# Last mixer of a stacked-block kernel: the query products and their rotations move behind those of keys and values

## The chip, the cores and the metric

The kernel runs on one core of one Trainium2 chip, as one program and one launch. The metric is the device time of that launch in microseconds. Three unprofiled runs of the kernel before took 3191.38, 3191.89 and 3195.28 us, so its median is 3191.89 us.

## The reference, cut to what matters

Two stacks of two blocks each run one after the other on 256 tokens of width 1024, all in float32. The change touches only the mixer of the last block, `odd_mixer`:

```python
p = h @ w_in                                   # (256, 1024) @ (1024, 2608)
q, kc, vc, ks, vs, kw, vw, gl = split(p)       # q: 16 heads of 64; the six others: 4 heads of 64
q, kc, ks, kw = rope(q), rope(kc), rope(ks), rope(kw)
gates = sigmoid(gl)                            # 3 for each head and token
k_cmp = compress(kc, pos[0], w1[0], ...)       # blocks of 32 tokens, stride 16: 15 blocks
v_cmp = compress(vc, pos[1], w1[1], ...)       # gelu((blocks + pos) @ w1 + b1) @ w2 + b2
o = gates_0 * att(q, k_cmp, v_cmp) + gates_1 * att(q, ks, vs) + gates_2 * att(q, kw, vw)
y = o @ w_out
```

With 256 tokens every one of the 4 selection blocks is chosen and the window covers everything, so the second and third branch are plain causal attention. Behind the mixer stand the last mixture of experts and a final norm.

## The kernel before, in words

Activations lie transposed: 8 chunks of 128 features on the partitions, 256 tokens along the free axis. Weights stream from HBM through a ring of 7 slots of 2 MB. SyncE issues the loads in the order in which `block(...)` was called while the program was planned, each as soon as the block 7 places ahead of it in that order has been read (`free_slot`, then `load`, L974). PSUM banks are handed out at planning time too: `fill_turn` goes round banks 0 to 3 for products, and `fill(b)` takes one of banks 4 to 7 for rotations and doubled keys. Every engine has its program written out by hand and runs it in order; semaphores join them. No scheduler rearranges anything, so the order of the calls in the TensorE, ScalarE and VectorE functions is the order on the chip.

One `unit` (L1053) is the product of 256 output features with all 256 tokens: 32 matmul records. Two `token_unit`s (L1068) are the product of the same size with tokens on the partitions, for values. The six products of one 256-column part of the weights are: kc and vc (one block, `od2.kc`, `od2.vc`), and for each of the selected and the window branch (`od2.kv[0]`, `od2.kv[1]`) one key unit and two token units. The queries take four units from two blocks (`od2.q`).

For a unit that needs rotary embedding, ScalarE copies the product into `z` (L1693, L1958), TensorE multiplies it by a fixed rotation matrix (`rotate`, L1420, 2 records), and VectorE combines the two in three operations (`rotary`, L2376, L2378, L2380). The rotated keys of a branch are then doubled into both halves of the partitions by TensorE (L1618, two banks of 4 records each) and copied to `kT` by ScalarE (L1967).

The compressed branch: VectorE writes the overlapping blocks plus the position term into `cmp_blk`, for kc and then vc: four times one memset (L2579) and four additions (L2584). TensorE multiplies them by the two halves of `w1` for kc and then vc (L1630, 128 records each, 60 moving columns a record), ScalarE applies gelu (L1973), and TensorE makes the second product (L1640 for keys, L1646 and L1649 for values). Attention follows: 48 jobs (16 heads by 3 branches), L1097 scores, L1108 transposes, L1121 values on TensorE, with softmax on VectorE and ScalarE.

The order on TensorE before is: norm sums, four query units, kc, vc, `rotate` of the queries, key and value products of both branches, the 48-column gate product (L1608), `rotate` of kc, `rotate` of kv[0], doubling of kv[0], `rotate` of kv[1], doubling of kv[1], compression, attention. On VectorE it is: rotary of the queries, the gate mask (L2574), rotary of kc, the compressed branch's blocks, rotary of kv[0], rotary of kv[1], attention.

Of the kernel before, what the change touches and what calls it, by code (L numbers as in the profile page):

```python
# [31 lines left out]
T = 256  # L32
# [165 lines left out]
def stacked_blocks_kernel(nc, A, consts_dram, counts_dram, slots_dram, out):  # L198
    with ExitStack() as ctx:
# [117 lines left out]
        def con(name):  # L317
            at, n = CONST[name]
            return const[:, at:at + n]
# [11 lines left out]
        bank_full = [sem(f"bank_full{b}") for b in range(8)]  # L331
# [13 lines left out]
        proj_ready = sem("proj_ready")  # L345
# [7 lines left out]
        rope_ready = sem("rope_ready")  # L353
        dup_ready = sem("dup_ready")
# [139 lines left out]
        pairs = []  # L494
# [164 lines left out]
        for i in range(4):  # L659
            b = block(col_load(A["od_pw1_w"][0], i * T, T), col_load(A["od_pw1_w"][0], D + i * T, T, T))  # L660
# [37 lines left out]
        for i, cap in enumerate(CAPS):  # L698
# [10 lines left out]
            if paired:  # L709
                st = paired_steps(lambda s, n: ([moe_col(s * HSTEP)], [moe_col(E1_FF + s * HSTEP)]),  # L710
                                  lambda s, n: [moe_row(s * HSTEP)], (0, 3) if i < 6 else (), scatter_fills)
# [102 lines left out]
        def rope_linear(W, c0, n):  # L814
            st = linear(W, c0, n, proj_ready)
            st.rots = [fill(4 + i % 4) for i in range(len(st.units))]
            st.rope = count(rope_ready, len(st.units))
            return st
# [36 lines left out]
        od2 = Stage()  # L855
        od2.norm = norm(moe2[0].h)
        QW, KW = NSA_H * HD, NSA_KV * HD
        od2.q = rope_linear(W3, 0, QW)
        b = block(col_load(W3, QW))
        fs = [fill_turn((proj_ready, count(proj_ready, 1) + 1)) for _ in range(2)]  # L860
        b.release = (bank_full[fs[1].b], fs[1].n)
# [5 lines left out]
        for i in range(2):  # L867
# [8 lines left out]
            st.dup_fills = [fill(4 + g, (dup_ready, count(dup_ready, 1) + 1)) for g in range(2)]  # L876
            od2.kv.append(st)
        od2.gate_fill = fill_turn((gates_ready, 1))
        od2.blk = count(cmp_ready, 2)
        od2.cmp = []  # L880
        for i in range(2):
# [154 lines left out]
        def _(pe):  # L1036
            def open_bank(f):

                if f.before is not None:
                    pe.wait_ge(*f.before.freed)  # L1040
                return PSB[f.b]

            def landed(b):
                pe.wait_ge(slot_landed[b.slot], b.landed)

            def unit(b, u, f, x, ready=None):

                ps = open_bank(f)
                for c in range(2):
                    for k in range(KD):  # L1050
                        if ready is not None and c == 0:
                            ready(k)
                        mm = nc.tensor.matmul(ps[:, c * T:(c + 1) * T],  # L1053
                                              kblk(b)[:, k, u * T + c * P:u * T + (c + 1) * P], x[:, k, :],
                                              start=k == 0, stop=k == KD - 1)
                mm.then_inc(bank_full[f.b], 1)

            def pe_linear(st, x, ready):
                for i, (b, u, f) in enumerate(st.units):
# [18 lines left out]
            def normed(st):  # L1078
                return lambda k: pe.wait_ge(xn_ready, st.xn + k + 1)
# [335 lines left out]
            def rotate(st, at_chunk):  # L1415

                for i, f in enumerate(st.rots):
                    pe.wait_ge(proj_ready, st.done + i + 1)
                    ps = open_bank(f)
                    nc.tensor.matmul(ps[:], con("rot"), z[:, at_chunk + 2 * i:at_chunk + 2 * i + 2, :],  # L1420
                                     start=True, stop=True).then_inc(bank_full[f.b], 1)
# [169 lines left out]
            pe_experts(moe2[0])  # L1591

            pe_norm(od2.norm)
            pe_linear(od2.q, xn, normed(od2.norm))
            landed(od2.kc.units[0][0])
            unit(*od2.kc.units[0], xn)
            unit(*od2.vc.units[0], xn)
            rotate(od2.q, 0)
            for i, st in enumerate(od2.kv):
                b, u, f = st.ku  # L1600
                landed(b)
                unit(b, u, f, xn)
                for b, c, f in st.vu:
                    token_unit(b, c, f, xn, KW, KW)
            ps = open_bank(od2.gate_fill)
            for c in range(TC):
                for k in range(KD):
                    mm = nc.tensor.matmul(ps[:, c * 3 * NSA_H:(c + 1) * 3 * NSA_H], xn[:, k, c * P:(c + 1) * P],  # L1608
                                          gate_w[:, k, :], start=k == 0, stop=k == KD - 1)
            mm.then_inc(bank_full[od2.gate_fill.b], 1)  # L1610
            rotate(od2.kc, 8)
            for i, st in enumerate(od2.kv):
                rotate(st, 12 + 2 * i)
                pe.wait_ge(rope_ready, st.rope + 1)
                for u, f in enumerate(st.dup_fills):
                    ps = open_bank(f)
                    for o in range(2):
                        mm = nc.tensor.matmul(ps[:, o * T:(o + 1) * T], con(f"dup{o}"), z[:, 12 + 2 * i + u, :],  # L1618
                                              start=True, stop=True)
                    mm.then_inc(bank_full[f.b], 1)  # L1620
            for i, st in enumerate(od2.cmp):
                pe.wait_ge(cmp_ready, od2.blk + 2)
                for b in st.blocks:
# [27 lines left out]
                mm.then_inc(bank_full[st.ofill.b], 1)  # L1651
            pe.wait_ge(cmp_ready, od2.cmp[1].out + 1)
            pe.wait_ge(dup_ready, od2.kv[1].dup + 2)
            pe_attention(od2.att)
            pe_linear(od2.out, mixed, lambda k: pe.wait_ge(mix_ready, od2.att.mix + k + 1))
            pe_experts(moe2[1])
# [10 lines left out]
        def _(act):  # L1667
            def full(f):
                act.wait_ge(bank_full[f.b], f.n)
                return PSB[f.b]  # L1670
# [16 lines left out]
            def copy_units(st, dst):  # L1687
                for i, (b, u, f) in enumerate(st.units):
                    d = dst(i)
                    ps = full(f)[:, 0:2 * T]  # L1690
                    if len(d.shape) == 3:
                        ps = ps.rearrange("p (c t) -> p c t", c=2)
                    nc.scalar.copy(d, ps).then_inc(f.freed[0], 1)  # L1693

            def pairs(x, at_chunk=0):
                return lambda i: x[:, at_chunk + 2 * i:at_chunk + 2 * i + 2, :]
# [253 lines left out]
            act_experts(moe2[0])  # L1950

            normalise(od2.norm)
            copy_units(od2.q, pairs(z))
            copy_units(od2.kc, pairs(z, 8))
            copy_units(od2.vc, pairs(z, 10))
            for i, st in enumerate(od2.kv):
# [5 lines left out]
            full(od2.gate_fill)  # L1962
            nc.scalar.activation(gates.rearrange("p c n -> p (c n)"), PSB[od2.gate_fill.b][:, 0:TC * 3 * NSA_H], ACT.Sigmoid)\
                .then_inc(gates_ready, 1)
            for i, st in enumerate(od2.kv):
                for u, f in enumerate(st.dup_fills):
                    nc.scalar.copy(kT[:, 4 * i + 2 * u:4 * i + 2 * u + 2, :],  # L1967
                                   full(f).rearrange("p (c t) -> p c t", c=2)).then_inc(dup_ready, 1)
            for i, st in enumerate(od2.cmp):
                ps = full(st.hfill)  # L1970
                NB = NSA_KV * NCMP
# [21 lines left out]
        def _(dve):  # L1993
# [15 lines left out]
            def full(f):  # L2009
                dve.wait_ge(bank_full[f.b], f.n)  # L2010
                return PSB[f.b]
# [360 lines left out]
            def rotary(st, at_chunk):  # L2372

                for i, f in enumerate(st.rots):
                    x = z[:, at_chunk + 2 * i:at_chunk + 2 * i + 2, :]
                    nc.vector.tensor_tensor(rot_tmp, full(f).rearrange("p (c t) -> p c t", c=2), twice(con("sin")),  # L2376
                                            ALU.mult).then_inc(bank_free[f.b], 1)
                    chain(nc.vector.tensor_tensor(x, x, twice(con("cos")), ALU.mult))  # L2378
                    freed(f)
                    nc.vector.tensor_tensor(x, x, rot_tmp, ALU.add).then_inc(rope_ready, 1)  # L2380
                    dve.wait_ge(rope_ready, st.rope + i + 1)
# [185 lines left out]
            dve_experts(moe2[0])  # L2567

            normalise(od2.norm, lambda k: scol[:, 1, 0, k:k + 1], lambda k: mod[:, 1, 0, k:k + 1])
            rotary(od2.q, 0)  # L2570
            dve.wait_ge(gates_ready, 1)
            for c in range(TC):
                g0 = gates[:, c, 0:3 * NSA_H:3]
                step(nc.vector.tensor_scalar(g0, g0, con("cmprow")[:, c:c + 1], None, ALU.mult))  # L2574
            rotary(od2.kc, 8)
            for i, pos in enumerate(("pos_k", "pos_v")):
                for o in range(2):
                    half, other = slice(o * HD, (o + 1) * HD), slice((1 - o) * HD, (2 - o) * HD)
# [6 lines left out]
                                cmp_blk[i][half, ls, o, c, :], src[:, :, a:a + NCMP],  # L2585
                                col(pos, a * CMP_S, CMP_S)[half].unsqueeze(2).to_broadcast([HD, CMP_S, NCMP]), ALU.add)
                ins.then_inc(cmp_ready, 1)
            for i, st in enumerate(od2.kv):
                rotary(st, 12 + 2 * i)
            dve_attention(od2.att)  # L2590
            add_chunks([f for b, u, f in od2.out.units], lambda k: mod[:, 1, 2, k:k + 1], ALU.mult)
            dve_experts(moe2[1])
# [33 lines left out]
```

## Time and profile before

| what | value |
|---|---|
| median of the runs | 3191.89 us |
| profiled execution | 3207.41 us, with a span of 3205.6 us |
| mean granted TensorE clock | 0.929 |
| TensorE busy | 2880.0 us (90% of the span), 15071 matmul records |
| VectorE busy | 797.5 us (25%) |
| ScalarE busy | 394.8 us (12%) |
| HBM | 641.64 MB read, 200 GB/s over the span |
| first unit of the last mixer starts | 2542.38 us |
| first compression product starts | 2649.14 us |
| attention of the last mixer starts | 2710.49 us |

A granted clock of 1.00 is TensorE at 2.4 GHz and 0.50 is 1.2 GHz; a value between the two is a stretch that holds both. Times of day below are microseconds from the start of the span. Idle time counts only where it stands on TensorE, the engine that nearly all of the chain of waits runs through.

### The profile page before, as it was taken

To read this page: it belongs to the slowest core of one execution; us is meant where nothing else is said; L and a number is where in the kernel's file an instruction comes from. 1 tells how busy PE (TensorE), PEld (TensorE's weight loads), DVE (VectorE), ACT (ScalarE), POOL (GpSimd) and SP (SyncE) were. 2 spreads that over 40 slices of the span, in tenths; PEclk is the share of its full clock that TensorE was granted. 3 is DMA by queue.
4 is the path that set the end of the run, shared out by engine and by line. 5 is a ranking of instruction groups with operands and counts; after the bars stand their busy time and mean duration, and the time that the engine had idled before them with its cause. 6 is when DMAs were issued, how large, how long until landed. Compare 5 with 4: busy or idle time off the path is not lost. (4 is left out here: it accounts for less than half of the span.)

```text
span 3205.6 us, 35329 instructions
## 1 busy us (share of the span) xinstructions
PE 2880.0 (90%) x15071; PEld 2201.0 (69%) x15071; DVE 797.5 (25%) x1968; ACT 394.8 (12%) x997; POOL 53.7 (2%) x67
## 2 busy tenths in 40 slices
PE   3999999979899999999997887796899989997998
PEld 3767888757778888888862332565878668566786
DVE  1211211882220202021111000344223221643112
ACT  1102000112200000000000000122100101432001
POOL 0000000600000000000000000000000000000000
PEclk9999999989899999999998999888899985788999
DMA  7333256420388888888889999300669830005462
GB/s 240 131 119 118 95 194 207 174 79 1 131 312 323 298 320 300 321 299 321 300 323 394 394 394 393 114 1 3 215 211 327 255 95 1 1 1 175 142 236 92
DMA packets 328577, 645.02 MB, mean 201 GB/s; under 512 B 12875, under 2 KB 98273, under 8 KB 328417
## 3 DMA queue, kind: packets, MB, share of 16 engines
q1 hardware_dynamic: 318608, 636.51, 55.1%
q10 hardware_dynamic: 9809, 6.21, 0.7%
q8 instruction: 121, 1.98, 0.3%
q14 instruction: 39, 0.32, 0.0%
HBM read 641.64 MB, written 1.05 MB: 200 GB/s over the span
## 5 line engine op out<-in xcount | busy, mean ns | idle before, releaser
L1160 PE MATMUL bank<-xn,ring 128*128 128x128 f32 (+3 forms) x6208 | 829.7, 296 | 7.2 <-issue 6.8
L1160 PEld LDWEIGHTS bank<-xn,ring 128*128 128x128 f32 x6208 | 797.0, 192 | 54.3 <-issue 22.2
L1053 PE MATMUL bank<-xn,ring 128*128 128x256 f32 x2048 | 462.9, 390 | 54.2 <-DVE xn L2563 17.7
L1053 PEld LDWEIGHTS bank<-xn,ring 128*128 128x128 f32 x2048 | 401.8, 197 | 115.8 <-issue 41.1
L2139 DVE TENSOR_TENSOR att<-att,bank 128x128 f32<-128x128 f32 (+2 forms) x162 | 48.6, 301 | 841.0 <-ACT att L1756 841.0
L1189 PE MATMUL bank<-ring,att 128*128 128x512 f32 (+1 forms) x560 | 246.1, 594 | 0.0
L1206 PE MATMUL bank<-ring,xn 128*64 128x512 f32 x336 | 175.9, 675 | 64.8 <-issue 64.8
L1189 PEld LDWEIGHTS bank<-ring,att 128*128 128x128 f32 (+1 forms) x560 | 101.9, 186 | 121.6 <-issue 121.6
L1210 PE MATMUL bank<-ring,xn 128*64 128x512 f32 x336 | 176.3, 676 | 0.0
L1206 PEld LDWEIGHTS bank<-ring,xn 128*64 128x64 f32 x336 | 48.5, 154 | 169.6 <-issue 168.4
L1756 ACT ACTIVATE att<-bank 128x128 f32<-128x128 f32 (+2 forms) x162 | 46.6, 288 | 873.7 <-PE bank L1160 873.7
L1390 PE MATMUL bank<-ring,att 128*128 128x512 f32 (+2 forms) x320 | 140.7, 595 | 0.0
L2186 DVE SCALAR_TENSOR_TENSOR sq<-ring,cs,sq 128x512 f32<-128x512 f32 x168 | 126.3, 752 | 6.0
L1160 PEld LDWEIGHTS bank<-sq,ring 128*128 128x128 f32 x1024 | 115.4, 192 | 4.9 <-issue 4.9
L1160 PE MATMUL bank<-sq,ring 128*128 128x128 f32 (+1 forms) x1024 | 115.6, 275 | 1.2 <-DMA ring<-moe_w_up 1.2
L1390 PEld LDWEIGHTS bank<-ring,att 128*128 128x128 f32 (+2 forms) x320 | 54.0, 173 | 74.5 <-issue 74.4
L2358 DVE TENSOR_TENSOR att<-att,bank 128x256 f32<-128x256 f32 (+3 forms) x64 | 18.8, 294 | 344.9 <-ACT att L1835 344.8
L2479 DVE SCALAR_TENSOR_TENSOR att<-z,cols,att 128x256 f32<-128x256 f32 x210 | 103.1, 562 | 1.1
L1086 PE MATMUL bank<-sq,ones 128*128 128x256 f32 x224 | 57.5, 416 | 48.0 <-ACT sq L1676 35.7
L2149 DVE TENSOR_TENSOR sq<-att,bank 64x512 f32<-64x512 f32 x21 | 14.5, 691 | 313.6 <-ACT att L1779 313.6
L1086 PEld LDWEIGHTS bank<-sq,ones 128*128 128x128 f32 x224 | 46.6, 211 | 57.7 <-issue 44.4
L1121 PE MATMUL bank<-att,vtok 128*64 128x256 f32 (+1 forms) x256 | 82.9, 465 | 0.0
(266 smaller groups left out, 2434.4 us busy)
## 6 DMA issues: line engine op xcount, KB each, us to landing
ring<-od_moe_gu SPq DMA_DIRECT2D x112, 2048.0 KB, 14.0
ring<-od_moe_down SPq DMA_DIRECT2D x56, 2048.0 KB, 18.4
ring<-ada_w SPq DMA_DIRECT2D x24, 2048.0 KB, 16.7
ring<-moe_w_gate SPq DMA_DIRECT2D x32, 1024.0 KB, 13.9
ring<-moe_w_up SPq DMA_DIRECT2D x32, 1024.0 KB, 12.2
ring<-moe_w_down SPq DMA_DIRECT2D x16, 2048.0 KB, 14.3
ring<-ev_w_in SPq DMA_DIRECT2D x10, 2048.0 KB, 18.8
ring<-ev_ffn_gu SPq DMA_DIRECT2D x10, 2048.0 KB, 13.0
```

Source lines behind the costliest of these rows:

```text
L1053: mm = nc.tensor.matmul(ps[:, c * T:(c + 1) * T], kblk(b)[:, k, u * T + c * P:u * T + (c + 1) * P], x[:, k, :], start=k == 0, stop=k == KD ...
L1086: mm = nc.tensor.matmul(ps[:, 0:T], ones[:], x[:, k, :], start=k == 0, stop=k == KD - 1)
L1121: mm = nc.tensor.matmul(ps[o:o + w, at_col:at_col + T], v, pT_att[0:kk, j.i % 2, m, :], start=j.start and m == 0, stop=j.stop and m == len ...
L1160: mm = nc.tensor.matmul(ps[:, half * T:half * T + w], kblk(b)[:, k, j * P:(j + 1) * P], src[:, k, 0:w], start=k == 0, stop=k == KD - 1)
L1189: mm = nc.tensor.matmul(PSB[f.b][0:st.width, :], hid[:, s % 2, j, 0:st.width], rblk(x.down)[:, j, half * 512:(half + 1) * 512], start=firs ...
L1206: ins = nc.tensor.matmul(ps[0:HP, :], xn[:, k, 0:HP], kblk(x.gate)[:, k, :], start=k == 0, stop=k == KD - 1)
L1210: mm = nc.tensor.matmul(ps[HP:P, :], xn[:, k, 0:HP], kblk(x.up)[:, k, :], start=k == 0, stop=k == KD - 1)
L1390: mm = nc.tensor.matmul(PSB[f.b][0:w, :], hid[:, n % 2, j, u0:u0 + w], rblk(x.down)[:, j, half * 512:(half + 1) * 512], start=x.first and ...
L1756: nc.scalar.activation(sg[:, i % 2, 0:w], ps[:, 0:w], ACT.Silu).then_inc(sg_ready, 1)
L2139: nc.vector.tensor_tensor(hj, sg[:, (x.at + j) % 2, 0:w], ps[:, T:T + w], ALU.mult)\
L2186: ins = nc.vector.scalar_tensor_tensor(y, w[:, k, :], cs[:, k:k + 1], y, ALU.mult, ALU.add)
L2479: ins = nc.vector.scalar_tensor_tensor(y, x, w, y, ALU.mult, ALU.add)
```

## The change

Planning: the two query blocks are loaded behind those of kc/vc, kv[0] and kv[1], and take their PSUM turns behind the gates. TensorE, ScalarE and VectorE follow the new order. Nothing is computed that wasn't before, and nothing is left out.

```diff
@@ planning
-        od2.q = rope_linear(W3, 0, QW)
         b = block(col_load(W3, QW))
...
         od2.gate_fill = fill_turn((gates_ready, 1))
+        od2.q = rope_linear(W3, 0, QW)
@@ TensorE
+            b, u, f = od2.kc.units[0]
+            landed(b)
+            unit(b, u, f, xn, normed(od2.norm))
+            unit(*od2.vc.units[0], xn)
+            key_value_units(od2.kv[0])
+            rotate(od2.kc, 8)
+            key_value_units(od2.kv[1])
+            rotate(od2.kv[0], 12)
...          (gate product, unchanged)
+            query_units(0, 1)
+            rotate(od2.kv[1], 14)
+            both_halves(od2.kv[0], 12)
+            query_units(1, 2)
+            both_halves(od2.kv[1], 14)
+            query_units(2, 4)
+            rotate(od2.q, 0)
             for i, st in enumerate(od2.cmp):
...
+            pe.wait_ge(rope_ready, od2.q.rope + 4)
             pe_attention(od2.att)
@@ ScalarE (behind the copies of kc, vc, kv[0], kv[1] and the sigmoid of the gates)
+            copy_query(0, 1)
+            copy_dup(0, od2.kv[0])
+            copy_query(1, 2)
+            copy_dup(1, od2.kv[1])
+            copy_query(2, 4)
@@ VectorE
-            rotary(od2.q, 0)
+            rotary(od2.kc, 8)
+            for i, st in enumerate(od2.kv):
+                rotary(st, 12 + 2 * i)
             dve.wait_ge(gates_ready, 1)
...          (gate mask; then, rotary of kc gone from here, the compressed branch's blocks)
-            for i, st in enumerate(od2.kv):
-                rotary(st, 12 + 2 * i)
+            rotary(od2.q, 0)
             dve_attention(od2.att)
```

`key_value_units(st)` is the key unit and the two token units of one branch. `both_halves(st, ...)` is the doubling (L1618) with its wait for VectorE's rotary of that branch. `query_units(a, b)` are query units a to b-1.

## Rows read from the trace of the kernel before

**Rows 1.** The page: TensorE's busy share, and its granted clock in 40 slices.
```profile
PE 2880.0 (90%) x15071; PEld 2201.0 (69%) x15071; DVE 797.5 (25%) x1968; ACT 394.8 (12%) x997; POOL 53.7 (2%) x67
PEclk9999999989899999999998999888899985788999
```
**Rows 2.** Chain of waits from 2542 us: start, duration, engine, tile, line, count.
```profile
2542.38 44.66 PE bank L1053 x192
2587.04 3.43 PE bank L1420 x8
2590.47 6.91 PE bank L1053 x32
...
2618.10 3.50 PE bank L1608 x32
2621.60 0.94 PE bank L1420 x2
2622.57 0.69 DVE sq L2376
...
2624.84 0.86 DVE memT L2579
...
2634.69 1.96 DVE att L2584 x4
...
2638.74 3.78 PE bank L1618 x8
2642.53 1.67 PE bank L1420 x2
...
2646.36 2.79 PE bank L1618 x8
2649.14 27.21 PE bank L1630 x128
...
2678.46 27.51 PE bank L1630 x128
...
2710.49 4.64 PE bank L1097 x14
```
**Rows 3.** Timeline by engine: TensorE's two waits (in brackets), one ScalarE copy.
```profile
2638.74 3.78 PE L1618 MATMUL bank<-z,const 128*128 128x256 f32 x8 [15.35 <-DVE z L2380]
2646.36 2.79 PE L1618 MATMUL bank<-z,const 128*128 128x256 f32 x8 [2.18 <-DVE z L2380]
2587.07 0.58 ACT L1693 COPY z<-bank 128x512 f32<-128x512 f32 x1 [6.32 <-PE bank L1053]
```
**Rows 4.** Instructions on the ring's tile, 2480 to 2640: compression weights' issues; landing times.
```profile
L974 SPq DMA_DIRECT2D ring<-od_cmp_w x8: 595/1921/4779, 2517.7 to 2573.9; - x8
DMA to landing us min/median/max: 7.5/12.6/20.0
```
**Rows 5.** Windows: length, busy PE, PEld, DVE, ACT, POOL (records), clock, DMA, GB/s.
```profile
2494.30:2508.70 14.40, 14.40 (x130) 14.40 (x130) 1.34 (x6) 1.22 (x4) 0.00 (x0) 1.00 0.95 353
...
2623.40:2638.70 15.30, 0.00 (x0) 0.00 (x0) 14.35 (x25) 0.00 (x0) 0.00 (x0) 0.62 0.00 0
...
2649.10:2676.30 27.20, 27.20 (x129) 27.05 (x127) 0.00 (x0) 1.87 (x2) 0.00 (x0) 0.50 0.00 1
...
2710.50:2717.50 7.00, 4.63 (x17) 3.54 (x17) 4.29 (x14) 3.71 (x12) 0.00 (x0) 0.50 0.00 0
2717.50:2738.50 21.00, 21.00 (x54) 11.28 (x55) 11.20 (x40) 8.04 (x29) 0.00 (x0) 0.50 0.00 0
2740.00:2760.00 20.00, 18.57 (x87) 10.50 (x87) 15.60 (x57) 12.01 (x42) 0.00 (x0) 1.00 0.00 1
...
2812.50:2830.00 17.50, 16.54 (x78) 9.34 (x76) 13.55 (x47) 10.60 (x37) 0.00 (x0) 1.00 0.01 1
```
**Rows 6.** Windows at the start of the second stack's first attention.
```profile
2127.00:2130.00 3.00, 2.77 (x14) 2.30 (x15) 1.80 (x6) 0.00 (x0) 0.00 (x0) 0.76 0.00 0
2130.00:2145.00 15.00, 12.40 (x33) 6.62 (x32) 10.25 (x28) 7.19 (x24) 0.00 (x0) 0.50 0.00 1
```

More of the change, by code:

```diff
@@ L1593, in _, with key_value_units @@
             pe_norm(od2.norm)
[L1594 to L1598, printed above, removed]
-            for i, st in enumerate(od2.kv):
+            def key_value_units(st):
                 b, u, f = st.ku
@@ L1604, in _, with both_halves, query_units @@
                     token_unit(b, c, f, xn, KW, KW)
+            def both_halves(st, at_chunk):
+                pe.wait_ge(rope_ready, st.rope + 1)
+                for u, f in enumerate(st.dup_fills):
+                    ps = open_bank(f)
+                    for o in range(2):
+                        mm = nc.tensor.matmul(ps[:, o * T:(o + 1) * T], con(f"dup{o}"), z[:, at_chunk + u, :],
+                                              start=True, stop=True)
+                    mm.then_inc(bank_full[f.b], 1)
+            def query_units(first, last):
+                for b, u, f in od2.q.units[first:last]:
+                    if u == 0:
+                        landed(b)
+                    unit(b, u, f, xn)
+            b, u, f = od2.kc.units[0]
+            landed(b)
+            unit(b, u, f, xn, normed(od2.norm))
[4 more added lines that the diff above has]
+            rotate(od2.kv[0], 12)
             ps = open_bank(od2.gate_fill)
@@ L1610, in _ @@
             mm.then_inc(bank_full[od2.gate_fill.b], 1)
[L1611 to L1620, printed above, removed]
+            query_units(0, 1)
[5 more added lines that the diff above has]
+            rotate(od2.q, 0)
             for i, st in enumerate(od2.cmp):
@@ L1952, in _, with copy_dup, copy_query @@
             normalise(od2.norm)
-            copy_units(od2.q, pairs(z))
+            def copy_dup(i, st):
+                for u, f in enumerate(st.dup_fills):
+                    nc.scalar.copy(kT[:, 4 * i + 2 * u:4 * i + 2 * u + 2, :],
+                                   full(f).rearrange("p (c t) -> p c t", c=2)).then_inc(dup_ready, 1)
+            def copy_query(first, last):
+                for i in range(first, last):
+                    b, u, f = od2.q.units[i]
+                    nc.scalar.copy(z[:, 2 * i:2 * i + 2, :], full(f).rearrange("p (c t) -> p c t", c=2))\
+                        .then_inc(proj_ready, 1)
             copy_units(od2.kc, pairs(z, 8))
@@ L1964, in _ @@
                 .then_inc(gates_ready, 1)
[L1965 to L1968, printed above, removed]
+            copy_query(0, 1)
[3 more added lines that the diff above has]
+            copy_query(2, 4)
             for i, st in enumerate(od2.cmp):
@@ L2574, in _ @@
                 step(nc.vector.tensor_scalar(g0, g0, con("cmprow")[:, c:c + 1], None, ALU.mult))
-            rotary(od2.kc, 8)
             for i, pos in enumerate(("pos_k", "pos_v")):
@@ L2587, in _ @@
                 ins.then_inc(cmp_ready, 1)
-            for i, st in enumerate(od2.kv):
-                rotary(st, 12 + 2 * i)
+            rotary(od2.q, 0)
             dve_attention(od2.att)
```

## The prediction, made before the changed kernel was run

> **What bounds the kernel now.** I read the page first. TensorE is busy for 90% of the span, and its clock stands near full except in a few slices, of which the lowest (5 and 7 tenths) are where the last mixer's compression and attention lie [rows 1]. A change to the order of work there can pay in two ways: by taking idle time off TensorE, and by changing the clock at which it works. So I read the chain of waits from the mixer's first unit on [rows 2]. It runs through TensorE without a break to 2622.5, and then leaves it: three VectorE operations of kc's rotary, then the compressed branch's blocks from 2624.84 to 2634.69 + 1.96 = 2636.65, and kv[0]'s rotary. Only then does TensorE double the first keys. The timeline gives the two waits by themselves: 15.35 us before the first doubling, 2.18 us before the second, both released by VectorE's last rotary operation [rows 3]. The reader is to see that VectorE stands in front of TensorE here because of the order of its own queue, not because it has much work: kv[0]'s rotary waits behind 11.8 us of blocks that nobody needs yet.
>
> Third, the windows [rows 5]. The wait takes the clock down (0.62 over it), and behind it the first compression product runs for 27.20 us, TensorE busy all the time, at 0.50. That is the larger find: the 60-column products stay at 1.2 GHz to the end of the compression, and attention begins at 0.50 as well.
>
> **The change part by part.** I lay the new order on TensorE with the durations of rows 2. A unit or a pair of token units is 6.91. The first unit is slow, since it starts behind the norm's wait: 44.66 - 5 x 6.91 = 10.11, and whatever unit stands first pays this, before and after. One rotation is 3.43 / 4 = 0.86. A doubling is 8 records of 256 columns, as in a unit, 6.91 / 32 x 8 = 1.73. The gates are 3.50.
>
> From 2542.38: kc ends at 2552.5, vc 2559.4, kv[0]'s three products 2573.2, rotation of kc 2574.1, kv[1]'s products 2587.9, rotation of kv[0] 2588.8, gates 2592.3, query unit one 2599.2, rotation of kv[1] 2600.0, doubling of kv[0] 2601.8, second query unit 2608.7, doubling of kv[1] 2610.4, two query units 2624.2, four rotations 2627.7. In one sum: 10.11 + 9 x 6.91 + 3 x 0.86 + 3.43 + 3.50 + 2 x 1.73 = 85.3. The first compression product then starts at 2627.7 instead of 2649.14 [rows 2]: **21.5 us** earlier. Of these 15.35 + 2.18 = 17.5 are the waits [rows 3], and 4.0 are work that ran at the low clock behind them (3.78 + 1.67 + 2.79 = 8.24 against 1.73 + 0.86 + 1.73 = 4.32).
>
> This holds only if no new wait arises, so each is checked. A rotary on VectorE takes at most 2624.84 - 2622.57 = 2.3 us [rows 2]. kv[0]'s is done at 2591.1 and wanted at 2600.0; kv[1]'s is done at 2602.3 and wanted at 2608.7. The gate mask and the blocks (11.8 us) follow from there and end near 2615; compression wants them at 2627.7, so they have 13 us to spare and lie beside the query products. If that cover were gone they would cost up to 11.8. The queries' rotary starts at about 2624.8 and ends by 2634; attention wants it 30 us later. A ScalarE copy takes 0.58 [rows 3]: the last query unit's is done near 2625.0, and its rotation, fourth in its row, starts at 2626.8. That is the tightest of all, with 1.8 us. Behind TensorE's added wait for the query rotary stands only attention. What is late next is therefore nothing on this stretch: TensorE bounds itself.
>
> SyncE's queue is the other thing the edit reorders. The five blocks of the input weights trade places at equal size. The compression weights' last issue is at 2573.9 [rows 4], on the release of the block in second place. That is kv[0]'s now, read by 2573.2, where it was the second query block, read by 2573.3. With the longest landing time of 20.0 it is there at 2594, and the second compression product wants it near 2644. Cost 0. Of the output weights one load goes out some 4 us later; attention hides it.
>
> **The clock behind it** is worth more than the wait. In the new order TensorE comes to the compression after 75 us without a wait, at 1.00. What are 60-column products worth then? The nearest rows are the experts' 64-column products with the same 128x128 weights: 128 records in 14.4 us, clock 1.00 to the end [rows 5]; this pattern stands in the trace four times, at 2472, 2494, 3128 and 3149. Bounds: half of 27.21, 13.6 us, and 27.21. I take 14.4: saved 27.21 - 14.4 = 12.8 and 27.51 - 14.4 = 13.1 [rows 2], together **25.9 us**, with 27.5 and 0 as the ends.
>
> The small products around the two gelus fill 5.8 us less the 0.52 of each gelu; at twice the clock they save between 0 and 2.5. I take **1**, since most of them are single short records with fixed gaps.
>
> The Trainium skill (TensorE: Matmul & The Clock Gate, "Why this matters for your kernels") says that TensorE gets its full clock by being kept busy, and loses it in idle gaps between bursts. The row of the first compression product is against this as the whole story: busy in 27.20 of 27.20 us, and 0.50 throughout [rows 5]. By that rule alone the new order would hold the full clock, the sum would be as here, and the rival of a low clock would get no chance; I give it a fifth because of this row.
>
> Attention starts at the low clock now. Until 2738.5 it makes 54 records in 21.0 us, 2.6 a us, and at full clock 87 in 20.0, 4.4 a us [rows 5]; so that stretch could shrink from 21.0 to 54 / 4.4 = 12.3, a gain of up to 8.7, if TensorE enters attention warm and stays so. Against it: the second stack's first attention came in at 1.00 and fell within its first microseconds, to stay at 0.50 for 15 us [rows 6], and the last mixer's opening has a like gap (4.63 busy of 7.00, rows 5). I take **2** of 0 to 8.7.
>
> Sum: 21.5 + 25.9 + 1 + 2 = 50.4 us. The profiled execution took 3207.41 for a span of 3205.6, so it would become 3157.0, span 3155.2. The runs' median lies 15.5 below the profiled one; I take the same difference off it: 3191.9 - 50.4 = **3141.5 us**.
>
> **The rivals.**
>
> *The compression stays at the low clock.* The same product shape held 0.50 for 27 us without a gap, and no long stretch of just this shape stands at 1.00. For it: rows 5, 2649.10. Against it: there the engine came in from the low clock. If this shape can't hold the level, 1 and 25.9 fall away and attention gains nothing: 3191.9 - 21.5 = 3170.4. Chance 0.19.
>
> *It falls in between.* Between the two products stand a gelu wait and 30-column records. If the clock goes there, 13.1 is lost, and attention's 2 with it: 3156.6. Chance 0.11.
>
> *A new wait takes the old one's place.* The copies, doublings and rotations are woven more tightly; if I have a dependence wrong, VectorE's 11.8 us of blocks stand before a doubling again, and the clock falls as it does now. Then 15.35 us of wait and the 4 behind it return, and the time is within 0.2% (6.4 us) of before. The order of VectorE's program speaks against it: both rotaries now stand ahead of the blocks. Chance 0.04.
>
> *Slower: attention at the low clock throughout.* Its three stretches at 1.00 (the first is 2740 to 2760, the last 2812.5 to 2830) last 57.5 us; at 2.6 records a us instead of 4.4 each takes 1.7 times as long, 40 us more. Attention's level changes several times within this one execution, so a shift in time may move it. The change becomes slower once the compression stays low and 21.5 / 0.7 = 31 us or more of these 57.5 are lost; all of them give 3191.9 - 21.5 + 40 = 3210. With the compression at full clock 50.4 can't be eaten up. Chance 0.03.
>
> **How the numbers follow.** My forecast gets 0.63, the rivals 0.19, 0.11, 0.04 and 0.03. The time is the forecast's, 3141.5; its own range is 3129 (13.6 us for each product, 2.5 for the small ones, 8.7 for attention give 3191.9 - 21.5 - 27.5 - 2.5 - 8.7 = 3131.7, less a little for luck in attention's later stretches) to 3152. The range to hold 8 in 10 takes in the two rivals of the clock: 3129 to 3172. No change means within 0.2%, about what a measurement of this kernel can tell. Faster: 0.63 + 0.19 + 0.11 = 0.93; same 0.04; slower 0.03.
>
> **What would show it.** Right: TensorE without a wait of more than 0.5 us from the first unit to the first compression product, which starts 85 us behind that unit; VectorE's blocks beside the query units; windows over the two products 14.4 long at 1.00. Wrong in the first step: a wait at L1618 or L1420. Wrong in the second: 27 us and 0.50 at L1630 with no wait before it. Whether attention opens at 1.00, and for how long, settles the last term.

## The result

Twenty runs of each kernel: the changed one has a median of 3167.80 us (3157.10 to 3193.19), the one before 3195.51 us (3191.38 to 3213.05). The ratio is 0.9917, 95% interval 0.9898 to 0.9936. The change is worth 27.7 us; 50.4 were forecast. The time lies inside the stated range, and the sign is right, but nearly half of the forecast gain is missing. The profiled execution took 3160.40 us, with a span of 3158.6 and a mean clock of 0.942. On its page the slices of the last mixer's compression and attention stand at 7 and 7 tenths, where they stood at 5 and 7 [rows 1]:

```profile
PE 2841.8 (90%) x15069; PEld 2175.4 (69%) x15071; DVE 797.0 (25%) x1968; ACT 395.4 (13%) x997; POOL 53.8 (2%) x67
...
PEclk9999999999899999999998999897899997798999
```

The chain of waits of the changed kernel, over the stretch of [rows 2] (start, duration, engine, tile, line, count):

```profile
2543.72 23.94 PE bank L1053 x96
2567.65 6.91 PE bank L1068 x32
2574.56 0.86 PE bank L1420 x2
...
2590.09 3.50 PE bank L1628 x32
...
2601.43 1.73 PE bank L1607 x8
2603.15 6.91 PE bank L1053 x32
2610.06 1.73 PE bank L1607 x8
2611.79 13.81 PE bank L1053 x64
2625.60 3.43 PE bank L1420 x8
2629.03 14.25 PE bank L1647 x128
...
2643.87 0.91 PE bank L1657 x16
2644.78 26.98 PE bank L1647 x128
...
2676.29 4.64 PE bank L1097 x14
```

L1607 is now the doubling (L1618 before), L1647 the compression product (L1630 before), L1628 the gates. TensorE goes from its first unit to the first compression product in 2629.03 - 2543.72 = 85.3 us, where it took 106.8. The doublings take 1.73 each, not 3.78 and 2.79 [rows 2]. All of TensorE's waits from 2540 to 2680 are these (engine, tile, line, what released it: us in total, times, longest):

```profile
PE bank L1053 <- DVE xn L2075: 7.1, 1, 7.1
PE bank L1657 <- ACT att L2003: 0.6, 1, 0.6
PE bank L1663 <- ACT att L2003: 0.6, 1, 0.6
PE bank L1097 <- ACT att L2012: 0.5, 1, 0.5
```

The 15.35 and 2.18 us of [rows 3] are gone, and nothing stands in their place. VectorE's timeline shows the blocks beside the query units, and the queries' rotary behind them:

```profile
2603.59 0.38 DVE L2606 TENSOR_SCALAR gates<-gates,const 128x16 f32<-128x16 f32 x2
2604.22 0.86 DVE L2610 MEMSET memT<- 64x960 f32 x1 [0.26 <-issue]
...
2614.17 1.97 DVE L2615 TENSOR_TENSOR att<-z,cols 64x240 f32<-64x240 f32 x4
2626.50 0.69 DVE L2406 TENSOR_TENSOR sq<-bank,const 128x512 f32<-128x512 f32 x1 [10.35 <-PE bank L1420]
```

The windows over the compression and attention of the changed kernel (columns as in [rows 5]; the clock is third from the end):

```profile
2629.00:2643.30 14.30, 14.27 (x129) 14.13 (x127) 5.48 (x9) 0.00 (x0) 0.00 (x0) 1.00 0.01 2
2643.30:2644.80 1.50, 0.93 (x17) 0.89 (x17) 0.00 (x0) 0.51 (x2) 0.00 (x0) 1.00 0.00 0
2644.80:2671.80 27.00, 26.95 (x128) 26.76 (x128) 0.00 (x0) 0.33 (x2) 0.00 (x0) 0.51 0.00 1
2676.30:2815.40 139.10, 130.51 (x512) 73.31 (x512) 93.40 (x336) 73.19 (x248) 0.00 (x0) 0.82 0.00 1
```

The first product held 1.00, as forecast. The second ran at the low clock, which came half a microsecond into it, just behind the 1.5 us between the two products: a gelu wait, in which TensorE is idle, and 16 records of 30 columns. And this profile is 47.0 us of span below the one before, far more than the medians' 27.7. So one profile of each does not stand for the two kernels: which execution was profiled can matter nearly as much as the change. That is what the experiments are about.

### The profile page after: what moved, and what is told of

Its sections match the earlier page's. It is cut to its first block and busy times, and to the rows that moved or that the text cites. A ratio compares the mean times of both kernels' runs of the same rounds, so it can differ in the third digit from the quotient of the medians.

```text
span 3158.6 us, 35329 instructions
## 1 busy us (share of the span) xinstructions
PE 2841.8 (90%) x15069; PEld 2175.4 (69%) x15071; DVE 797.0 (25%) x1968; ACT 395.4 (13%) x997; POOL 53.8 (2%) x67
## 5 line engine op out<-in xcount | busy, mean ns | idle before, releaser
L1206 PE MATMUL bank<-ring,xn 128*64 128x512 f32 x336 | 171.1, 658 | 69.8 <-issue 69.8
L1210 PE MATMUL bank<-ring,xn 128*64 128x512 f32 x336 | 171.5, 660 | 0.0
L1774 ACT ACTIVATE att<-bank 128x128 f32<-128x128 f32 (+2 forms) x162 | 46.7, 288 | 873.8 <-PE bank L1160 873.8
L1086 PE MATMUL bank<-sq,ones 128*128 128x256 f32 x224 | 57.8, 416 | 48.5 <-ACT sq L1694 36.3
L2179 DVE TENSOR_TENSOR sq<-att,bank 64x512 f32<-64x512 f32 x21 | 14.5, 691 | 313.8 <-ACT att L1797 313.8
L1086 PEld LDWEIGHTS bank<-sq,ones 128*128 128x128 f32 x224 | 46.6, 211 | 58.5 <-issue 45.0
## 6 DMA issues: line engine op xcount, KB each, us to landing
ring<-moe_w_down SPq DMA_DIRECT2D x16, 2048.0 KB, 14.3
```

The costliest lines, as they stand in the source:

```text
L1086: mm = nc.tensor.matmul(ps[:, 0:T], ones[:], x[:, k, :], start=k == 0, stop=k == KD - 1)
L1206: ins = nc.tensor.matmul(ps[0:HP, :], xn[:, k, 0:HP], kblk(x.gate)[:, k, :], start=k == 0, stop=k == KD - 1)
L1210: mm = nc.tensor.matmul(ps[HP:P, :], xn[:, k, 0:HP], kblk(x.up)[:, k, :], start=k == 0, stop=k == KD - 1)
```

## The experiments

Theory A: the clock falls because of gaps between products (idle time, or the small records that stand there; no run separates the two). Theory B: the 60-column products can't hold it. A question behind both: does one profile stand for a kernel here? Ratios are to the kernel before on the same chip, with 95% intervals; where a run is set against the changed kernel, the two were on different chips, unless said otherwise.

**The two compression products back to back** (`back_to_back`). `compress_hidden` is the 128-record product alone, taken out of the loop:

```diff
-            for i, st in enumerate(od2.cmp):
+            def compress_hidden(i, st):
                 pe.wait_ge(cmp_ready, od2.blk + 2)
...          (the 128 records, unchanged)
+            for i, st in enumerate(od2.cmp):
+                compress_hidden(i, st)
+            for i, st in enumerate(od2.cmp):
                 pe.wait_ge(cmp_ready, st.hid + 2)
```

> The changed kernel with both compression products (128 records each) one straight behind the other, so that the first gelu and the small records behind it no longer stand between them. Theory A (the clock falls because of the gap and the small records between the two products): the second product takes about 14.3 us at a granted clock of 1.00, the stage to attention shrinks by some 13 us against the changed kernel, and the time is about 13 us below it, that is some 40 us below the kernel before. Theory B (the clock falls because the 60-column products themselves can't hold it for long): it falls some 16 us after the first product begins, gap or none, the second product takes about 26 us, and the time stays at the changed kernel's, 27 us below the kernel before, within 3 us.

Median 3156.4 us against 3199.5, ratio 0.9868 (0.9832 to 0.9904), 43 us below. The windows over both products together, and over attention:

```profile
2624.80:2653.30 28.50, 28.50 (x258) 28.44 (x256) 5.46 (x9) 0.51 (x2) 0.00 (x0) 1.00 0.01 1
2658.00:2802.30 144.30, 136.16 (x513) 75.99 (x513) 93.62 (x336) 73.00 (x248) 0.00 (x0) 0.78 0.00 1
```

60-column products held the full clock for 28.5 us with nothing between them, and so they did in each of the four profiles of kernels that have them back to back (this one, `both`, `filler`, `all_filled`; in the last three the records are 120 columns wide). That refutes B as it was put: the 27 us at 0.50 of [rows 5] do not follow from the shape alone.

**120 moving columns instead of 60** (`wide`); the further 60 are thrown away.

```diff
-                        mm = nc.tensor.matmul(ps[:, fc * NB:(fc + 1) * NB], w1[...],      (shortened)
-                                              cmp_blk[i][:, l].rearrange("p o c n -> p (o c n)"),
+                        two = min(2, CMP_L - l)
+                        mm = nc.tensor.matmul(ps[:, fc * T:fc * T + two * NB], w1[...],   (shortened)
+                                              cmp_blk[i][:, l:l + two].rearrange("p l o c n -> p (l o c n)"),
```

> The changed kernel with 120 moving columns instead of 60 in each of the 256 compression records (the further 60 columns are computed and thrown away); gap and order as in the changed kernel. Theory A (gap): the clock falls in the gap as before, first product 14.3 us, second about 27 us, time as the changed kernel within 3 us. Theory B (shape): the clock holds through the gap or comes back within a few us of it, second product 14.3 to 18 us, time 9 to 13 us below the changed kernel. A record of 120 columns at full clock should cost no more than one of 60 (128-column records stand at 0.113 us each in the experts); if it does, the first product shows it by more than 14.5 us.

Median 3156.3, ratio 0.9875 (0.9833 to 0.9917). In the profile the clock came through the same gap:

```profile
2625.80:2640.00 14.20, 14.20 (x128) 14.08 (x127) 5.44 (x9) 0.00 (x0) 0.00 (x0) 1.00 0.01 2
2640.00:2641.50 1.50, 0.90 (x18) 0.85 (x17) 0.00 (x0) 0.51 (x2) 0.00 (x0) 1.00 0.00 0
2641.50:2656.00 14.50, 14.46 (x129) 14.32 (x128) 0.00 (x0) 0.32 (x2) 0.00 (x0) 1.00 0.00 1
```

By itself this looks like B. But a later profile of the unwidened changed kernel came through the gap too (below), so it is not shown that the width did it. Doubling the columns cost nothing: 14.2 us either way. The profiled executions of `back_to_back` and `wide` were also the fastest of their six (9 and 14 us below their medians), so they do not show what the usual execution does.

**The kernel before with its waits filled** (`before_filled`): the clock's part without the schedule's.

```diff
                 rotate(st, 12 + 2 * i)
+                ps = open_bank(st.dup_fills[0])
+                for n in range((35, 5)[i]):
+                    nc.tensor.matmul(ps[:, 0:T], con("rot"), xn[:, n % KD, :], start=True, stop=True)
                 pe.wait_ge(rope_ready, st.rope + 1)
```

> The kernel before, with 35 and 5 products of 256 columns put into TensorE's two waits for VectorE's rotaries; they are thrown away and nothing else changes, so the order of the work and the 17.5 us of the waits stay. This gives the clock's part without the schedule's. Theory A or B alike: 4 us less on the doublings and rotation, 13 us less on the first compression product: 17 us below the kernel before, or 10 us more than that if attention profits too. A rival, that the whole gain of the change is the 17.5 us of removed waits and the clock gives nothing: time as the kernel before within 3 us.

Median 3192.3 against 3199.5, ratio 0.9970 (0.9946 to 0.9993): 7 us, not 17. The profile does what was expected: the filled wait at 1.00 and the first product in 14.2 us. The gain is small all the same. A reason that fits is that the kernel before often has this product at full clock already, and two of its four profiles below do.

```profile
2626.00:2641.00 15.00, 14.87 (x69) 12.73 (x68) 14.06 (x25) 0.00 (x0) 0.00 (x0) 1.00 0.00 1
2648.10:2662.30 14.20, 14.20 (x128) 14.07 (x127) 0.00 (x0) 1.87 (x2) 0.00 (x0) 1.00 0.00 1
```

**A wait put ahead of the compression in the changed kernel** (`stall`).

```diff
             rotate(od2.q, 0)
+            pe.wait_ge(rope_ready, od2.q.rope + 4)
             for i, st in enumerate(od2.cmp):
```

> The changed kernel with TensorE's wait for the query rotary moved ahead of the compression, so that it stands idle for about 5.5 us there. Both theories on the gap alike: the clock falls in that idle time and both products run at 0.50, 27 us each. Against the changed kernel: 5.5 of wait and 13 for the first product, 18 us slower, some 9 us below the kernel before. If the clock survives the wait: 5.5 us slower only.

Median 3193.2, ratio 0.9982 (0.9958 to 1.0007): 6 us below the kernel before, where some 9 were expected, and the interval holds no difference. In the profile 5.5 us of idle time took the clock down and cost 13 us more behind it (27.5 instead of 14.3):

```profile
2642.00:2647.50 5.50, 0.00 (x0) 0.00 (x0) 5.28 (x9) 0.00 (x0) 0.00 (x0) 0.90 0.00 1
2647.50:2675.00 27.50, 27.49 (x128) 27.38 (x128) 0.00 (x0) 0.00 (x0) 0.00 (x0) 0.50 0.00 1
```

This profile lies 18.6 us above the median of its kernel's runs. Part of its length has nothing to do with the edit: 12.3 us were lost in one of the experts' 64-column products ahead of the mixer, which entered at 1.00 behind a wait for a load, lost the clock about a microsecond later and took 26.67 us, where the next one of the same shape took 14.40 (timeline; in brackets the wait before it and what ended it):

```profile
2471.39 26.67 PE L1160 MATMUL bank<-sq,ring 128*128 128x64 f32 x128 [1.57 <-DMA ring<-moe_w_up]
```

In the first profiles of both kernels the same product stands behind a wait of 1.2 and 1.3 us and keeps 1.00 (14.5 us). So a fall of the clock behind a wait of a microsecond or two, for the whole of the product that follows, is not peculiar to the compression.

The Trainium skill (TensorE: Matmul & The Clock Gate, "Why this matters for your kernels") asks for no long idle gaps between bursts of products. `stall` and `back_to_back` agree: 27.5 us at 0.50 behind 5.5 us of idle time, 28.5 us at 1.00 without a gap. The changed kernel shows more than that row says: its clock also fell behind a gap with only 0.6 us of idle time in it.

**VectorE's order undone alone** (`blocks_first`).

```diff
-            for i, st in enumerate(od2.kv):
-                rotary(st, 12 + 2 * i)
             dve.wait_ge(gates_ready, 1)
...
+            for i, st in enumerate(od2.kv):
+                rotary(st, 12 + 2 * i)
             rotary(od2.q, 0)
```

> The changed kernel with one part undone: on VectorE the gate mask and the compressed branch's blocks stand ahead of the rotaries of both key branches again; TensorE and ScalarE keep the new order. If the gain needs VectorE's order: the blocks then run from the gates on, from about 50 us behind the first unit to 62, kv[0]'s rotary ends at about 65, TensorE wants it at 57: a wait of about 7 us before the first doubling and a clock that falls there, to come back during the query units. Then 7 to 10 us slower than the changed kernel, 17 to 20 below the kernel before. If the query products alone are cover enough: no wait and the changed kernel's time within 3 us.

TensorE waits, by its timeline, for the time expected, and its first doubling is slow again:

```profile
2608.24 3.78 PE L1607 MATMUL bank<-z,const 128*128 128x256 f32 x8 [7.14 <-DVE z L2410]
```

The compression starts 95.7 us behind the first unit instead of 85.3, and the profile took 3170.4 us where the changed kernel's took 3160.4: 10 us. Its runs do not show this: the median is 3170.0 (ratio 0.9920, interval 0.9893 to 0.9946), 28 us below the kernel before, where 17 to 20 were expected and the changed kernel has 27.7. They scatter over 24 us. So the VectorE half of the edit removes a 7 us wait by the trace, and its worth in the runs stays unmeasured.

**Both edits of the compression together** (`both`).

> The changed kernel with the two compression products back to back and with 120 moving columns in each record. Theory A+B together (either of the two keeps the clock by itself, as the two traces showed): the compression takes 28.5 us at 1.00, no more is won than with one of them, 40 us below the kernel before. If either one fails in some executions, the two together are steadier: 43 to 46 us below, and a narrower spread of the runs.

Median 3158.7, ratio 0.9865 (0.9840 to 0.9890), 40 us below the kernel before, as expected: no more than either alone, 28.5 us at 1.00. Its five runs lie within 9 us, those of `back_to_back` within 16 and those of `wide` within 38. Its attention had the same 144.3 us at 0.78 as that of `back_to_back`.

**Attention's waits filled** (`filler`, on top of `both`).

```diff
                 def turned(j):
-                    pe.wait_ge(prob_ready, st.prob + j.i + 1)
                     ps = open_bank(j.t_fill)
+                    if st is od2.att:
+                        for n in range(5 if j.i == 0 else 1 if j.i % 3 == 1 else 0):
+                            nc.tensor.matmul(ps[:, 0:T], con("rot"), con("cos"), start=True, stop=True)
+                    pe.wait_ge(prob_ready, st.prob + j.i + 1)
```

> The kernel with both edits and, in the last mixer's attention alone, thrown-away products of 256 columns in TensorE's waits for the softmax: five at the opening, one in each third job (16), some 9 us of work laid into about as much idle time. Over the six traces so far attention took 119 us + 0.40 us for each us at the low clock (47.8 to 87.4 us of it). If idle time is what takes the clock down there: at the low clock less than 20 us, attention 122 to 128 us instead of 138 to 145, 10 to 16 us below the kernel with both edits. If the shape of attention's products is the cause: the clock falls as often, and the time is 0 to 9 us above it.

Median 3136.8 (3136.0 to 3138.6) against 3198.2, ratio 0.9799 (0.9774 to 0.9823): 22 us below `both`, on the same chip, more than expected, and the runs lie within 2.6 us. Between the two profiles, of which that of `both` was the fastest of its runs, it is 14.5 us, all of it in attention, which took 128.9 us instead of 144.3:

```profile
2662.30:2791.20 128.90, 122.98 (x555) 73.72 (x555) 94.45 (x336) 72.89 (x248) 0.00 (x0) 0.96 0.00 1
```

**The same in each kernel, to take attention's level out of the comparison** (`before_att`, `after_att`).

> The kernel before with the thrown-away products in the waits of the last mixer's attention alone (five at the opening, one in each third job). Theory (attention's level is what makes the runs of both kernels differ): attention takes 129 to 132 us instead of 153.4 in the profile, the runs lie within a few us of each other instead of 20, and their median is 10 to 20 us below the kernel before. Rival (the spread comes from elsewhere): 0 to 5 us below, spread as before.

> The changed kernel with the same products in the last mixer's attention. Against before_att this gives the change's own worth with attention's level taken out of both: 21.5 us of schedule and clock up to the compression, 13 for the first compression product, 0 to 1 for the second: 34 to 36 us, with little spread. If the change's gain came in part from attention's level it is less here than between the two plain kernels' profiles (47 us), and if the plain medians (28 us) are the whole of it, it stays at 28.

`before_att`: median 3169.6 (3167.1 to 3171.4), ratio 0.9908 (0.9889 to 0.9927), attention 128.5 us instead of 153.4. `after_att`: median 3152.0 (3145.7 to 3165.2), ratio 0.9862 (0.9835 to 0.9888). So filling attention's waits alone took 28 us off the kernel before, more than the 10 to 20 expected, and left its runs within 4.3 us of each other, which refutes the rival for that kernel. The runs of `after_att` still lie 20 us apart; in the new order attention's level is not the whole of the spread. The difference between the two kernels is 17.5 us, half of the 34 to 36 expected. The windows say why. Compression products of `before_att`, first and second:

```profile
2650.00:2664.70 14.70, 14.69 (x128) 14.55 (x127) 0.00 (x0) 1.87 (x2) 0.00 (x0) 0.97 0.00 1
2666.20:2692.10 25.90, 25.89 (x129) 25.70 (x128) 0.00 (x0) 0.31 (x1) 0.00 (x0) 0.53 0.00 1
```

and of `after_att`:

```profile
2631.30:2645.60 14.30, 14.27 (x129) 14.13 (x127) 5.49 (x9) 0.00 (x0) 0.00 (x0) 1.00 0.01 2
2647.20:2674.70 27.50, 27.50 (x128) 27.31 (x128) 0.00 (x0) 0.31 (x1) 0.00 (x0) 0.50 0.00 1
```

The old order with its 15 us wait has the first product at full clock too. With the clock of the compression and of attention nearly alike, what is left is the waits and the slow doublings: of the 17.6 us between the spans of the two profiles 21.5 stand between the first unit and the compression, the compression gives back 1.3, and 2.8 stand against the change ahead of the first unit, where the kernels do the same.

**Further profiles of both plain kernels** (`before_look2` to `before_look4`, `after_look2` to `after_look4`).

> The kernel before once more, for one look at how its attention's level varies between executions: if the pattern is fixed by how attention is entered, 87 us of 153 at the low clock again and 3205 to 3210; if it varies, another share, and a time near 3195.

> The kernel before, a third look. If the execution that the prediction was read from was the odd one: first compression product near 14.4 us at 1.00, second 26 to 27.5, attention 153 us, time 3190 to 3200. If both patterns are common: 27 us for the first product again, 3205 to 3213.

> The kernel before, a fourth look; the same two outcomes as in the third.

> The changed kernel once more, for one look. If the fall of the clock between the two compression products is the rule: first product 14.3 us, second 27 us again. If it is chance: 14.3 us for both, or 27 for both. Time 3157 to 3175.

> The changed kernel, a third look. Two looks gave 14.25 and 27 us for the two compression products and 139 us of attention with 51 us at the low clock, at 3157 to 3160, under the runs' median of 3168. If the median's 8 us lie in attention: 145 to 160 us of it with 70 to 100 at the low clock, the compression as before. If they lie in the compression: 27 us for the first product too.

> The changed kernel, a fourth look; the same outcomes as in the third.

With the first profile of each there are four of each. All in us; "compression" runs from the start of the first product to that of attention, and the starts are those of the chain of waits:

| | run | first unit to compression | compression | attention | attention's clock |
|---|---|---|---|---|---|
| before | 3207.4 | 106.8 | 61.4 | 153.4 | 0.72 |
| before_look2 | 3196.2 | 105.3 | 46.7 | 153.2 | 0.72 |
| before_look3 | 3196.6 | 105.3 | 46.7 | 153.2 | 0.72 |
| before_look4 | 3201.4 | 106.8 | 61.4 | 144.2 | 0.78 |
| after | 3160.4 | 85.3 | 47.3 | 139.1 | 0.82 |
| after_look2 | 3159.2 | 85.3 | 47.3 | 139.2 | 0.82 |
| after_look3 | 3175.8 | 83.9 | 48.4 | 148.7 | 0.75 |
| after_look4 | 3159.0 | 83.8 | 34.1 | 148.9 | 0.74 |

In its compression the kernel before comes in two kinds, two profiles each. `before_look2` is the kind that the prediction did not see (first product, second product, attention):

```profile
2651.20:2665.60 14.40, 14.40 (x129) 14.28 (x127) 0.00 (x0) 1.87 (x2) 0.00 (x0) 0.99 0.00 1
2667.10:2693.30 26.20, 26.20 (x129) 26.05 (x128) 0.00 (x0) 0.31 (x1) 0.00 (x0) 0.53 0.00 1
2697.90:2851.10 153.20, 146.54 (x513) 80.80 (x513) 93.69 (x336) 72.95 (x248) 0.00 (x0) 0.72 0.00 1
```

What the clock did between the two doublings can be read in short windows, of the first profile of the kernel before:

```profile
2642.50:2645.00 2.50, 1.68 (x3) 0.16 (x1) 0.72 (x2) 0.58 (x1) 0.00 (x0) 0.70 0.00 0
2645.00:2647.50 2.50, 1.15 (x5) 1.04 (x6) 1.27 (x2) 0.00 (x0) 0.00 (x0) 0.98 0.01 3
2647.50:2650.00 2.50, 2.50 (x10) 2.13 (x9) 0.00 (x0) 1.39 (x3) 0.00 (x0) 0.50 0.00 0
```

and of `before_look2`, where the second doubling begins 1.4 us later from the start of the span:

```profile
2645.50:2648.00 2.50, 0.32 (x2) 0.29 (x2) 1.98 (x3) 0.00 (x0) 0.00 (x0) 1.00 0.01 3
2648.00:2651.00 3.00, 3.00 (x8) 2.33 (x8) 0.00 (x0) 0.58 (x1) 0.00 (x0) 0.50 0.00 0
2651.20:2654.20 3.00, 3.00 (x29) 3.00 (x27) 0.00 (x0) 1.87 (x2) 0.00 (x0) 0.96 0.02 5
```

In both the clock came back after the first doubling, before TensorE's second wait (2.18 us), and fell again within the second doubling. In the first profile the doubling had 1.7 us left to run when it fell, and the compression then stayed at 0.50 to its end. In `before_look2` the doubling had 3.2 us left (it took 3.50 instead of 2.79 us), the clock came back as the compression began, and the product had 0.99. A difference of 1.5 us in where the fall stands against the end of the doubling goes with 13 us behind it; why the clock came back in the one and not in the other is not shown.

`after_look4` held the clock through the gap between the products, with 60 columns:

```profile
2626.80:2641.00 14.20, 14.20 (x128) 14.07 (x127) 5.43 (x9) 0.00 (x0) 0.00 (x0) 1.00 0.01 2
2642.50:2657.00 14.50, 14.46 (x129) 14.32 (x128) 0.00 (x0) 0.32 (x2) 0.00 (x0) 1.00 0.00 1
```

**The best version** (`all_filled`): `filler` with 15 thrown-away products before the first key unit, 2 before the gelu of the values and 1 before attention.

> The best kernel so far (changed kernel, compression products back to back and 120 columns wide, attention filled) with thrown-away products in three more of TensorE's waits: 15 before the first key unit, behind the norm; 2 before the gelu of the values; 1 before attention. If a wait's idle time is what takes the clock down in each: the first unit takes 7 instead of 10 us, attention opens at 1.00: 4 to 6 us below the kernel with attention filled alone, 64 to 67 us below the kernel before. If not, 0 to 2 us above it.

Median 3129.3 (3128.6 to 3131.2) against 3197.2, ratio 0.9783 (0.9762 to 0.9804): 68 us below the kernel before. The norm's wait stays at 1.00 with thrown-away products in it, the first unit takes 7 us instead of 10, and attention runs at 1.00 to its end:

```profile
2537.00:2544.60 7.60, 7.00 (x34) 5.85 (x32) 6.46 (x11) 0.42 (x1) 0.00 (x0) 1.00 1.12 213
2544.60:2552.00 7.40, 7.40 (x35) 6.52 (x36) 2.07 (x7) 0.26 (x1) 0.00 (x0) 1.00 0.95 180
...
2660.00:2785.00 125.00, 118.44 (x555) 70.40 (x554) 94.23 (x336) 72.81 (x248) 0.00 (x0) 1.00 0.00 1
```

## Why the prediction was wrong

The failed step is the one headed "The clock behind it", 25.9 us for two compression products at full clock, over a base in which both ran at 0.50. The profiles show 9.4 us in its place, since the first product was often at full clock before the change and the second rarely behind it.

- *The waits and the doublings, 21.5 us.* Right: the four profiles of each kernel average 106.0 and 84.6 us from first unit to compression, 21.5 apart. In the first profile of the changed kernel the order of events on TensorE, VectorE and SyncE came out within a microsecond of the working once the later start is allowed for, the covers held, and no new wait arose.
- *First product, 12.8 us.* Its time in the changed kernel was right (14.25 against 14.4 from [rows 5]); its time in the kernel before was not. The 27.21 of [rows 2] is that of two profiles in four; the other two had 14.4. So it was worth 6.6 us in the mean of the profiles, not 12.8. The base was one execution, taken for the kernel. The prediction noted that this profile lay 15.5 us above the median of the runs, and carried the difference along unexplained; that was the sign.
- *Second product, 13.1 us.* Not won in three profiles of four (26.98, 26.99 and 27.51 us; the fourth 14.45), so worth 2.9 us in the mean: the clock fell among the small records between the products or within a microsecond behind them. The rival "It falls in between" named the place, at 0.11; it was the common case. The experts' 64-column rows had no such gap inside them. Of the profiles that come to the gap at full clock in the changed order, with 60 columns (these four, `blocks_first` and `after_att`), five of six lost the clock there, and of the four without the gap none did. Only one of those four, `back_to_back`, has 60 columns, but its runs go the same way (43 us below the kernel before, where the changed kernel is 27.7 below). So the gap is the likely cause, and its idle time and its small records are not told apart.
- *The small products, 1 us.* [rows 2] give 6.6 us for them and the gelu waits, where the prediction worked with 5.8. All that is not the two products went from 6.3 to 6.0 us in the mean of the profiles: 0.3.
- Over the profiles the compression went from 54.0 to 44.3 us: 9.7, against 25.9 + 1.
- *Attention, 2 us.* 151.0 against 144.0, 7 us, with more difference among the profiles of one kernel than between the means of the two, so that no gain of the change is shown. It opened at 0.50 in both, where the change could have made it enter at full clock.
- *The rival of the low clock.* Its reason (this shape) is refuted, though its time, 3170.4, is the nearest of all. That is luck in part: it takes 21.5 us off a base of 3191.9, and the runs show 27.7 off one of 3195.5. `after_att` against `before_att` does come out near the 21.5 alone: 17.5 us once attention's level is out.

In the profiles the clock of the compression is what fell short, by 17 us; the terms without the clock came out. What stays open: the eight profiles differ by 36.8 us in the mean where twenty runs each differ by 27.7 in the median, so four profiles do not give the shares of the kinds, and some 9 us of what the runs lack are assigned to nothing. Four of the changed kernel's twenty runs took 3187 to 3193, and no profile caught one. Both products low (as in `stall`) would add 13 us to a usual run, and a low experts' product ahead of the mixer, which the profile of `stall` has, 12; that they are of either kind is not shown. In `after_look3` and `after_look4` the stretch behind attention took 347 us instead of 343. Most of that stands in its last products, again by the clock: the final norm's sums (L1086) took 6.05 us in `after_look3` and 3.72 in the first profile.

## What to carry to other kernels

Where TensorE's clock is at stake, a wait can cost its length plus what runs at half clock behind it, and whether it does so can depend on a microsecond: take several profiles before a forecast counts it, and ask why a profile lies above its median, in which stretch, and whether that stretch has to do with the change at all. Here a gap of 1.5 us between two dense stretches was worth closing by order of work. Where waits can't be closed, thrown-away products in them can pay (22 us here in the medians for some 9 us of them in attention, 14.5 in the profiles), and in three of the four kernels that had them in attention the runs came within 5 us of each other.

## What of the hardware was not expected

- The last mixer's attention, the same instructions in all these kernels, takes 137.7 to 153.8 us where its waits are not filled, and the clock goes with it: 0.72 gives 153, 0.74 and 0.75 give 149, 0.78 gives 144, 0.82 gives 139. With 21 thrown-away products in its waits and 3 ahead of it, it stood at 1.00 and took 125. The low clock lasts 20 us and more there while TensorE is busy without a break ([rows 5], 2717.50); with the 21 short products in its waits the granted clock was 0.96 to 0.97 over all of it.
- These levels of attention came back to within 0.2 us in different executions, and in different kernels (144.3 and 144.2 at 0.78; 139.1 three times at 0.82). The clock's course looks like a few fixed patterns rather than noise. What chooses among them is not shown: `before` and `before_look4` have the same compression and the same opening of attention (4.64 us for its first 14 records), and then 153.4 and 144.2 us.
- A product of 64 columns in the experts, entered at full clock, took 26.67 us instead of 14.40 behind a wait of 1.57 us, TensorE busy all the time (`stall`).
- Products of 120 columns took the time of products of 60 (128 records in 14.2 us).
